# Two u tiles moved behind the convolved channels, first z columns split early, merging stage's loads by chunk

## The chip, the cores and the metric

One core of one Trainium2 chip runs the whole program. The metric is the device time of one execution in microseconds (us), and less is better. TensorE is called PE, VectorE DVE, ScalarE ACT, GpSimd POOL, and SyncE SP; SP only issues transfers.

## What is computed

Two model blocks run one after the other on 1024 tokens of 1024 features, in float32. The change touches the first projection of the first block and the merging stage of the second. Cut to what matters:

```python
# first block: projection of the normed tokens (and of 256 context tokens), 5168 columns
u, zf, zs, xbc, dt_raw = split(h @ w_in)             # 512, 512, 1536, 2560, 48 columns
xbc = silu(depthwise_conv_3x3(xbc) + conv_b)         # 16 x 64 grid of tokens; 3 taps for the context
four = fourier_mixer(u, zf, ...)                     # u as it is, z through silu
# second block: merging
merged = sigmoid(g_fox + b) * (out_fox @ w_proj_fox) + sigmoid(g_dsa + b) * (out_dsa @ w_proj_dsa)
x = x + gate * (merged @ w_out)                      # then norm, scale and shift, and the router
```

## The kernel before

`project_first` holds the normed tokens, turned, in two float32r parts (`hh` high, `hl` low); a product of two split operands takes three matmuls (`three`). Weights are split alike: high is a copy in float32r, low is the raw value less high.

**The channels' stage** (`project_channels`) makes 24 tiles of 128 columns, two for each piece of 256 columns that SP brings into a ring of three buffers (`Ring`) and that POOL splits (`Splits.part`) into one of two weight buffers. POOL may split piece g when both tiles of piece g-2 are summed. Tiles 0 to 3 are the u columns (`scalar_u` copies a sum out and stores it). Tiles 4 to 23 are the channels c = 0 to 19 of xbc: PE sums the tile, ACT copies it into a padded image (`scalar`), DVE makes the nine taps of the grid and three of the context (`vector`), ACT applies silu and stores (`scalar_silu`), PE turns the result in tensor_turn (two tiles later, between the first and second 512 tokens of a sum) and ACT copies that out (`scalar_turn`). Images and results have two buffers each. At the stage's end all engines wait for all of its signals, stores included.

**The z stage** (`project_tokens`) makes 4 groups of 512 z columns by 8 token tiles. SP brings 512 columns (2 MB), ACT splits off high, DVE makes low (`split`), PE sums with hh and hl stationary and the weights moving. Beside it DVE weighs 14 pieces of modulation weights (`weigh`), and PE adds each up with one matmul (`add_up`) after two z tiles. The splits of groups 1 to 3 stand ahead of a `weigh` on DVE.

**The merging stage** (`merge`, some 1,900 us later) works through 8 token tiles: PE projects `oT` (attention results, `ofoxT` and `odsaT`) with `wp`, DVE multiplies by the gates `gs` (POOL adds the bias `bg`, ACT takes the sigmoid), DVE adds both halves (line 2165), PE turns the sum, projects the next tile and closes this one with `wo`. At its start POOL issues the weights' loads (8 MB in three transfers) and SP issues `bg` and four broadcast rows before `oT`, `gs` and `x` of the first tile. Each engine works off its own instructions in the order of the code; nothing reorders them.

Of the kernel before, what the change touches and what calls it, by code (L numbers as in the profile page):

```python
# [357 lines left out]
class Splits:  # L358


    def __init__(self, core, s, ring):
        self.core, self.ring = core, ring
        self.w = [[s.sb(f"w1_{k}{b}", [P, KD, 256], R32) for k in ("high", "low")] for b in range(2)]
        self.halves, self.parted, self.summed = s.sem("w1_high_done"), s.sem("w1_split"), s.sem("xbc_summed")

    def part(self, g):
# [4 lines left out]
        split_on_pool(self.core, self.w[g % 2][0][:], self.w[g % 2][1][:], ring.raw[p % 3][:], self.halves).then_inc(*self.parted.up())  # L371


def project_channels(core, dram, tables, taps, ring, splits, hh, hl, ready):

# [4 lines left out]
    with Stage(core) as s:  # L380
        img = [s.sb(f"img{b}", [P, GRID_H + 2, GRID_W + 2]) for b in range(2)]
        line = [s.sb(f"line{b}", [P, CTX + 2]) for b in range(2)]
        acc, res = ([s.sb(f"{k}{b}", [P, TOK]) for b in range(2)] for k in ("acc", "res"))
        xt = [s.sb(f"xt{b}", [P, NT + NC, P]) for b in range(2)]
        zeroed, evicted, activated = s.sem("img_zeroed"), s.sem("xbc_evicted"), s.sem("xbc_silu_done")
        tapped, conv = s.sem("tap_done"), s.sem("conv_done")
        xturned, xout = s.sem("xt_turned"), s.sem("xt_copied")
# [15 lines left out]
        def tensor(n):  # L403
# [4 lines left out]
            if n >= 6:  # L408
                tensor_turn(n - 6)
            last = part(n, 1, 512, 512)  # L410
            if n >= 4:
# [24 lines left out]
        def scalar_u(n):  # L436
            s_ = n % 2
            act.wait_ge(*summed.at(n + 1))
            if n >= 2:
                act.wait_ge(*u_stored[s_].at(n // 2))  # L440
            act.activation(res[s_][:, 0:SEQ], flat2(core.bank[:, 3 * s_:3 * s_ + 2, :]), ACT.Copy).then_inc(*evicted.up())
            act.wait_ge(*evicted.at(n + 1))
            act.dma_start(dram["uT"][P * n:P * n + P, :], res[s_][:, 0:SEQ]).then_inc(*u_stored[s_].up())

        def scalar(c):
            s_, n = c % 2, c + 4
# [11 lines left out]
        def scalar_silu(c):  # L458
# [5 lines left out]
            else:  # L464
                act.wait_ge(*u_stored[s_].at(2))
# [23 lines left out]

        for g in range(12):  # L490
            if g + 1 < 12:
                splits.part(g + 1)
                if g + 3 < 12:
                    ring.load(ring.PIECES + g + 3, parted.at(g + 1))
            for n in (2 * g, 2 * g + 1):
                tensor(n)
                if n < 4:
                    scalar_u(n)
                else:
                    scalar(n - 4)  # L500
                    if n > 4:
                        scalar_silu(n - 5)
                    vector(n - 4)
        scalar_silu(NCT - 1)
        for c in (NCT - 2, NCT - 1):
            tensor_turn(c), scalar_turn(c)


def project_tokens(core, dram, tables, cs, hh, hl):
# [4 lines left out]
    with Stage(core) as s:  # L514
        raw = s.sb("zw_raw", [P, KD, 512])
        zw = [[s.sb(f"zw_{k}{b}", [P, KD, 512], R32) for k in ("high", "low")] for b in range(2)]
# [3 lines left out]
        aw, acc = [s.sb(f"mod_w{b}", [P, KD // 2, 512]) for b in range(2)], s.sb("mod_acc", [P, 512])  # L520
        bias, out = (s.sb(f"mod_{k}", [1, 512]) for k in ("bias", "out"))
        raw_in, high_done, parted = s.dma("zw_raw_in"), s.sem("zw_high_done"), s.sem("zw_split")
# [6 lines left out]
        def sync(i):  # L529
            if i:  # L530
                sp.wait_ge(*parted.at(i))
            sp.dma_start(raw[:], win[:, :, COL_Z + 512 * i:COL_Z + 512 * i + 512]).then_inc(*raw_in.up())

        def split(i):
            act.wait_ge(*raw_in.at(i + 1))
            if i >= 2:
                act.wait_ge(*summed.at(NT * (i - 1)))
            act.activation(zw[i % 2][0][:], raw[:], ACT.Copy).then_inc(*high_done.up())
            dve.wait_ge(*high_done.at(i + 1))
            dve.tensor_tensor(zw[i % 2][1][:], raw[:], zw[i % 2][0][:].bitcast(F32), ALU.subtract).then_inc(*parted.up())  # L540

        def tensor(n):
            i, m = n // NT, n % NT
            if m == 0:
                pe.wait_ge(*parted.at(i + 1))
            if n >= 4:
                pe.wait_ge(*gated.at(n - 3))
            products(pe, core.bank[:, n % 4, :], [p for k in range(KD) for p in three(
                *(a[:, k, P * m:P * m + P] for a in (hh, hl)), *(a[:, k, :] for a in zw[i % 2]))]).then_inc(*summed.up())
# [12 lines left out]
        def fetch_mod(q):  # L562
            w_name, b_name, _, _, at = mods[q]
            cols = slice(512 * at, 512 * at + 512)
            for half in range(2):
                if q:
                    sp.wait_ge(*weighed.at(KD * q - 4 + 4 * half))
                sp.dma_start(aw[half][:], dram[w_name].rearrange("(p k) n -> p k n", k=KD)[:, 4 * half:4 * half + 4, cols]).then_inc(*aw_in[half].up())
# [19 lines left out]
        def add_up(q):  # L588
            pe.wait_ge(*weighed.at(KD * q + KD))
            if q:  # L590
                pe.wait_ge(*added.at(q))
# [32 lines left out]
        sync(0), split(0), sync(1)  # L624
# [17 lines left out]
def project_first(core, dram, tables):  # L642
    with Stage(core) as s:
        hh, hl = (s.sb(k, [P, KD, TOK], R32) for k in ("h_high", "h_low"))
        cs = s.sb("mod_silu", [P, KD, 3])
        with Stage(core) as s1:
            taps, ring = s1.sb("taps", [P, 10 * NCT]), Ring(core, s1, dram)
            splits = Splits(core, s1, ring)
            ready = front(core, dram, tables, cs, taps, ring, hh, hl, lambda: splits.part(0))
            project_channels(core, dram, tables, taps, ring, splits, hh, hl, ready)  # L650
        project_tokens(core, dram, tables, cs, hh, hl)

# [2106 lines left out]
```

## Time and profile before

| | us |
|---|---|
| median of 3 runs | 3400.55 (3399.44 to 3404.88) |
| profiled execution | 3398.51, span 3396.3 |
| PE busy | 2863.1 (84%) |
| DVE busy | 2118.6 (62%) |
| ACT busy | 1235.3 (36%) |
| POOL busy | 535.3 (16%) |

The span is that of the instructions in one profiled execution; its own device time is 2.2 us longer, and the median of the runs another 2.0 us. The shares are means over stages with different limits, so the time of a change is read in its own stage. All places in time below are us from the start of the span.

### The profile page before, as it was taken

To read this page: it belongs to the slowest core of one execution; us is meant where nothing else is said; L and a number is where in the kernel's file an instruction comes from. 1 tells how busy PE (TensorE), PEld (TensorE's weight loads), DVE (VectorE), ACT (ScalarE), POOL (GpSimd) and SP (SyncE) were. 2 spreads that over 40 slices of the span, in tenths; PEclk is the share of its full clock that TensorE was granted. 3 is DMA by queue.
4 is the path that set the end of the run, shared out by engine and by line. 5 is a ranking of instruction groups with operands and counts; after the bars stand their busy time and mean duration, and the time that the engine had idled before them with its cause. 6 is when DMAs were issued, how large, how long until landed. Compare 5 with 4: busy or idle time off the path is not lost.

```text
span 3396.3 us, 34380 instructions
## 1 busy us (share of the span) xinstructions
PE 2863.1 (84%) x12552; PEld 2126.6 (63%) x12552; DVE 2118.6 (62%) x2906; ACT 1235.3 (36%) x2024; POOL 535.3 (16%) x320
## 2 busy tenths in 40 slices
PE   7999959979588699879889958795988479999992
PEld 3777746755466444468767847684444368888882
DVE  6399945526688523344726979841222479999985
ACT  3122221110366511122224126572211067777772
POOL 1422100000111100001200045452110011111101
PEclk9999979989788799989999969897999689999996
DMA  6333237534455432134442164114324289999995
GB/s 204 102 103 109 88 130 257 192 127 137 164 187 177 159 135 75 44 112 119 114 122 72 72 144 89 26 41 169 117 75 157 97 316 412 416 412 414 412 389 217
DMA packets 259104, 586.24 MB, mean 173 GB/s; under 512 B 27189, under 2 KB 158245, under 8 KB 241650
## 3 DMA queue, kind: packets, MB, share of 16 engines
q1 hardware_dynamic: 185618, 449.00, 36.9%
q0 software_dynamic: 29968, 64.18, 6.4%
q10 hardware_dynamic: 43344, 70.79, 5.6%
q8 instruction: 103, 1.69, 0.2%
q14 instruction: 71, 0.58, 0.1%
HBM read 463.26 MB, written 120.65 MB: 172 GB/s over the span
## 4 chain that ended last, share of the span: by engine, by line


## 5 line engine op out<-in xcount | busy, mean ns | idle before, releaser
L2413 DVE TENSOR_TENSOR e_low<-e_raw,e_high 128x4096 fp32r<-128x4096 f32 x99 | 438.0, 4426 | 69.5 <-ACT e_high L2407 69.4
L2407 ACT ACTIVATE e_high<-e_raw 128x4096 fp32r<-128x4096 f32 x99 | 359.5, 3633 | 32.8 <-DVE live L2364 26.4
L128 PE MATMUL banks<-p_w_high,p_high 128*128 128x512 f32 (+1 forms) x640 | 250.1, 391 | 18.1 <-DVE p_w_low L1526 18.1
L128 PE MATMUL banks<-p_w_low,p_high 128*128 128x512 f32 (+1 forms) x640 | 245.8, 384 | 0.0
L128 PE MATMUL banks<-p_w_high,p_low 128*128 128x512 f32 (+1 forms) x640 | 245.1, 383 | 0.0
L128 PE MATMUL banks<-c_w,c_mT 128*128 128x512 f32 x512 | 225.9, 597 | 9.0 <-DMA c_w<-in_w_out 9.0
L128 PE MATMUL banks<-e_high,e_xhigh 128*128 128x512 f32 x528 | 211.1, 400 | 10.0 <-issue 7.2
L483 DVE SCALAR_TENSOR_TENSOR acc<-img,taps,acc 128x1024 f32<-128x1024 f32 x160 | 209.8, 1311 | 5.7
L128 PE MATMUL banks<-h_high,w_high 128*128 128x512 f32 (+1 forms) x544 | 201.0, 370 | 9.2 <-POOL w_low L355 4.5
L128 PE MATMUL banks<-e_high,e_xlow 128*128 128x512 f32 x528 | 207.9, 394 | 0.0
L128 PE MATMUL banks<-e_low,e_xhigh 128*128 128x512 f32 x528 | 207.2, 392 | 0.0
L128 PE MATMUL banks<-h_low,w_high 128*128 128x512 f32 (+1 forms) x544 | 198.2, 364 | 0.0
L128 PE MATMUL banks<-h_high,w_low 128*128 128x512 f32 (+1 forms) x544 | 198.1, 364 | 0.0
L128 PE MATMUL banks<-m_wp,m_oT 128*128 128x512 f32 x256 | 126.3, 656 | 60.7 <-DMA m_oT<-odsaT 36.0
L128 PEld LDWEIGHTS banks<-c_w,c_mT 128*128 128x128 f32 x512 | 96.5, 192 | 122.8 <-issue 113.1
L1423 DVE TENSOR_SCALAR_CACHE_REDUCE c_rows<-c_rows,i_cand 128x384 bf16<-128x384 f32 (+5 forms) x186 | 169.0, 944 | 2.2
L2544 POOL DMA_INDIRECT e_x<-h,ids x33 | 87.8, 2661 | 500.1 <-PE banks L138 458.2
L1998 POOL TENSOR_TENSOR a_P<-a_P,a_rc 128x256 f32<-128x256 f32 (+7 forms) x64 | 135.1, 2111 | 122.2 <-DVE a_rc L1990 121.6
L128 PEld LDWEIGHTS banks<-p_w_high,p_high 128*128 128x128 f32 x640 | 123.3, 193 | 40.6 <-issue 18.5
L1093 PE MATMUL banks<-s_xf,s_M 128*128 128x64 f32 x768 | 107.3, 305 | 47.9 <-DVE s_M L1050 25.4
L1093 PEld LDWEIGHTS banks<-s_xf,s_M 128*128 128x128 f32 x768 | 107.2, 222 | 59.2 <-issue 26.6
L128 PEld LDWEIGHTS banks<-p_w_high,p_low 128*128 128x128 f32 x640 | 123.1, 192 | 23.9
(452 smaller groups left out, 6127.5 us busy)
## 6 DMA issues: line engine op xcount, KB each, us to landing
e_raw<-in_exp_w SPq DMA_DIRECT2D x99, 2048.0 KB, 10.6
mod_w<-in_ada_w SPq DMA_DIRECT2D x24, 1024.0 KB, 6.1
s_sums<-cumT SPq DMA_DIRECT2D x32, 768.0 KB, 5.2
s_X<-xtok SPq DMA_DIRECT2D x19, 1024.0 KB, 7.4
p_raw<-in_w_in SPq DMA_DIRECT2D x18, 1024.0 KB, 6.5
y<-e_y ACTq DMA_DIRECT2D x33, 512.0 KB, 10.9
xbcT<-res ACTq DMA_DIRECT2D x20, 640.0 KB, 2.9
xtok<-xt ACTq DMA_DIRECT2D x20, 640.0 KB, 3.7
```

Source lines behind the costliest of these rows:

```text
L128: last = pe.matmul(out, a, b, start=start and n == 0, stop=stop and n == len(pairs) - 1)
L483: dve.scalar_tensor_tensor(out=grid, in0=src, scalar=wt, in1=grid, op0=ALU.mult, op1=ALU.add).then_inc(*tapped.up())
L1093: pe.matmul(core.bank[:, y0, HP * h:HP * h + HP], M[n % 2][w][:, h, :], xfs[c % 2][w][:, c0:c0 + HP], start=h == 0 and w == 0, stop=False)
L1423: dve.tensor_scalar(self.junk[n][:, 0:P * (j + 1)], self.score[j], threshold, 0.0, op, ALU.add, accum_out=count).then_inc(*self.found.up())
L1998: pool.tensor_tensor(both, both, over(rc[b][:], 2, L), ALU.mult).then_inc(*scaled.up())
L2407: act.activation(self.high[p % HIGHS][:], self.raw[p % RAWS][:], ACT.Copy).then_inc(*self.high_done.up())
L2413: dve.tensor_tensor(self.low[p % HIGHS][:], self.raw[p % RAWS][:], self.high[p % HIGHS][:].bitcast(F32), ALU.subtract).then_inc(*self.low_ ...
L2544: pool.indirect_dma_start(out=x[b][:], out_offset=None, in_=dram["h2"], in_offset=bass.IndirectOffsetOnAxis(ap=ids[:, m:m + 1].bitcast(U32 ...
```

## The change

In the channels' stage the order of tiles becomes u 0, u 1, channels 0 to 19, u 2, u 3. The ring goes on with pieces 12 and 13, the first 512 z columns; POOL splits piece 12, and after the last u tile ACT and DVE split piece 13 (`split_last`), both into the channels' weight buffers. PE no longer waits at the stage's end, and the z stage starts on those buffers. Later z groups are loaded and split in halves of 256 columns, and the z matmuls read 512 columns as two runs of 256. In the merging stage ACT issues `wp` in 8 chunks of 512 KB and `wo` after the first sigmoid; SP issues `oT` and `gs` of tile 0 first, then `bg`, `x` and the four rows. (A function `fourier` is added that nothing calls.)

```diff
-            col = 256 * g if g < 2 else COL_XBC + 256 * (g - 2)
+            col = 0 if g == 0 else COL_XBC + 256 * (g - 1) if g < 11 else 256 if g == 11 else COL_Z + 256 * (g - 12)
...
+    CONVS = range(2, 2 + NCT)
-    with Stage(core) as s:
+    with Stage(core, (dve, act, pool, sp)) as s:
...
-            if n >= 6:
-                tensor_turn(n - 6)
+            if 4 <= n < 2 * 12 - 1:
+                tensor_turn(n - 4)
...
+        def split_last():
+            act.wait_ge(*ring.here(ring.PIECES + 13))
+            act.wait_ge(*summed.at(24))
+            for k in (0, 4):
+                act.activation(w[1][0][:, k:k + 4, :], ring.raw[(ring.PIECES + 13) % 3][:, k:k + 4, :], ACT.Copy).then_inc(*z_high.up())
+                dve.wait_ge(*z_high.now())
+                dve.tensor_tensor(w[1][1][:, k:k + 4, :], ring.raw[...][:, k:k + 4, :], w[1][0][:, k:k + 4, :].bitcast(F32),
+                                  ALU.subtract).then_inc(*splits.last_split.up())
...
+                if n in CONVS:
+                    scalar(n - 2)
+                    if n > 2:
+                        scalar_silu(n - 3)
+                    vector(n - 2)
+                elif n == 22:
+                    scalar_turn(NCT - 2), scalar_u(n), scalar_silu(NCT - 1)
+                else:
+                    scalar_u(n)
+        split_last()
+        tensor_turn(NCT - 1), scalar_turn(NCT - 1)
...
         def split(i):
-            act.activation(zw[i % 2][0][:], raw[:], ACT.Copy).then_inc(*high_done.up())
-            dve.tensor_tensor(zw[i % 2][1][:], raw[:], zw[i % 2][0][:].bitcast(F32), ALU.subtract).then_inc(*parted.up())
+            for b in range(2):
+                act.activation(zw[i % 2][:, b, 0], raw[b][:], ACT.Copy).then_inc(*high_done.up())
+                dve.tensor_tensor(zw[i % 2][:, b, 1], raw[b][:], zw[i % 2][:, b, 0].bitcast(F32), ALU.subtract).then_inc(*parted.up())
...
-        pool.dma_start(wp[0][:], weights("w_proj_fox_2")).then_inc(*weights_in[0].up())
-        pool.dma_start(wp[1][:], weights("w_proj_dsa_2")).then_inc(*weights_in[1].up())
-        pool.dma_start(wo[:], weights("w_out_2")).then_inc(*weights_in[2].up())
+        for j, name in enumerate(("w_proj_fox_2", "w_proj_dsa_2")):
+            for k in range(4):
+                act.dma_start(wp[j][:, k, :], dram[name][P * k:P * k + P, :]).then_inc(*weights_in[j].up())
...
-        bring(0), bring_x(0)
+        bring(0), bring_x(0), bring_rows()
+        act.dma_start(wo[:], weights("w_out_2")).then_inc(*weights_in[2].up())
```

Three places show the order. The first is ACT from the image of channel 19 to the second z tile; `res` is a silu, `xt` a turned tile, `zo` a z tile. Before:

```order
L454 ACTIVATE img<-banks 128x16x64
L456 ACTIVATE line<-banks 128x256
L466 ACTIVATE res<-acc,taps 128x1280
L468 DMA xbcT<-res 128x1280
L466 ACTIVATE res<-acc,taps 128x1280
L468 DMA xbcT<-res 128x1280
L431 ACTIVATE xt<-banks 128x512 x2
L431 ACTIVATE xt<-banks 128x256
L434 DMA xtok<-xt 128x10x128
```

After the change, from the copy-out of u tile 2 on (`u_out`; `w` is a channels' weight buffer):

```order
L447 ACTIVATE u_out<-banks 128x1024
L449 DMA uT<-u_out 128x1024
L470 ACTIVATE res<-acc,taps 128x1280
L472 DMA xbcT<-res 128x1280
L447 ACTIVATE u_out<-banks 128x1024
L449 DMA uT<-u_out 128x1024
L499 ACTIVATE w<-w_raw 128x1024 x2
L437 ACTIVATE xt<-banks 128x512 x2
L437 ACTIVATE xt<-banks 128x256
L440 DMA xtok<-xt 128x10x128
L582 ACTIVATE zo<-banks 128x512
```

The last silu now stands between two u tiles, and both copies of the z split stand ahead of the last turned tile's copies. The second place is SP at the start of the merging stage, before:

```order
L2108 DMA m_bg<-in_b_gate 128x2048
L2108 DMA m_gate<-mod 128x1024
L2108 DMA m_gain<-in_norm_g 128x1024
L2108 DMA m_m<-mod 128x1024
L2108 DMA m_shift<-mod 128x1024
L2131 DMA m_oT<-ofoxT 128x4x128
L2131 DMA m_oT<-odsaT 128x4x128
L2134 DMA m_gs<-proj 128x2048
```

and after the change:

```order
L2284 DMA m_oT<-ofoxT 128x4x128
L2284 DMA m_oT<-odsaT 128x4x128
L2287 DMA m_gs<-proj 128x2048
L2289 DMA m_bg<-in_b_gate 128x2048
L2300 DMA m_xin<-x 128x1024
L2259 DMA m_gate<-mod 128x1024
L2259 DMA m_gain<-in_norm_g 128x1024
L2259 DMA m_h<-mod 128x1024
L2259 DMA m_shift<-mod 128x1024
L2284 DMA m_oT<-ofoxT 128x4x128
```

The attention results and gates went ahead of 3 MB of broadcast rows, of which 1 MB (`bg`) is still needed before the first gate. The third place is ACT there after the change, where the weights' transfers came in from POOL's queue:

```order
L2253 DMA m_wp<-in_w_proj_fox 128x1024 x4
L2253 DMA m_wp<-in_w_proj_dsa 128x1024 x4
L2294 ACT_TABLE_LOAD
L2294 ACTIVATE m_gs<-m_gs 128x2048
L2380 DMA m_wo<-in_w_out 128x8x1024
L2294 ACTIVATE m_gs<-m_gs 128x2048
```

`wo` stands behind the first sigmoid, which waits for `gs`, `bg` and POOL's add.

## Rows read from the trace of the kernel before

**Rows 1.** By stretch: busy PE, PEld, DVE, ACT, POOL; clock, DMA share, GB/s.
```profile
180.00:413.00 233.00, 222.14 (x1182) 184.27 (x1181) 227.86 (x174) 57.96 (x84) 58.12 (x14) 1.00 0.29 98
...
2350.00:2360.00 10.00, 0.00 (x0) 0.00 (x0) 1.22 (x1) 0.00 (x0) 0.00 (x0) 0.50 1.03 405
```
**Rows 2.** Waits of PE, 485 to 700: us in total, times, longest us.
```profile
PE banks L592 <- DVE mod_acc L586: 9.7, 3, 4.0
```
**Rows 3.** Timeline of PE, 443 to 486: start, us, what, idle before.
```profile
460.76 0.69 PE L138 MATMUL banks<-mats,res 128*128 128x128 f32 x2 [12.77 <-ACT xt L431]
```
**Rows 4.** Timeline of ACT in the channels' stage: copies of sums, silu.
```profile
124.69 1.03 ACT L441 ACTIVATE res<-banks 128x1024 f32<-128x1024 f32 x1 [10.13 <-PE banks L128]
138.70 1.03 ACT L454 ACTIVATE img<-banks 128x1024 f32<-128x1024 f32 x1 [12.98 <-PE banks L128]
...
380.50 1.03 ACT L454 ACTIVATE img<-banks 128x1024 f32<-128x1024 f32 x1 [8.04 <-PE banks L128]
...
401.47 1.36 ACT L466 ACTIVATE res<-acc,taps 128x1280 f32<-128x1280 f32 x1 [3.90 <-DVE acc L487]
413.13 1.03 ACT L454 ACTIVATE img<-banks 128x1024 f32<-128x1024 f32 x1 [8.04 <-PE banks L128]
...
444.29 1.03 ACT L454 ACTIVATE img<-banks 128x1024 f32<-128x1024 f32 x1 [8.08 <-PE banks L128]
```
**Rows 5.** Timelines of DVE and of POOL around one split.
```profile
303.48 0.75 DVE L480 TENSOR_SCALAR acc<-img,taps 128x1024 f32<-128x1024 f32 x1
...
315.10 4.22 DVE L487 SCALAR_TENSOR_TENSOR acc<-line,taps,acc 128x256 f32<-128x256 f32 x2
319.25 5.07 DVE L480 TENSOR_SCALAR acc<-img,taps 128x1024 f32<-128x1024 f32 x1
...
315.38 3.66 POOL L353 TENSOR_TENSOR w_high<-w_raw,zero 128x2048 fp32r<-128x2048 f32 x1 [24.23 <-PE banks L128]
```
**Rows 6.** Timelines of ACT, DVE and PE from the last store to z.
```profile
464.92 0.38 ACTq L434 DMA_DIRECT2D xtok<-xt  x1
477.13 3.62 ACT L538 ACTIVATE zw_high<-zw_raw 128x4096 fp32r<-128x4096 f32 x1 [12.24 <-DMA zw_raw<-in_w_in]
...
480.88 4.42 DVE L540 TENSOR_TENSOR zw_low<-zw_raw,zw_high 128x4096 fp32r<-128x4096 f32 x1 [22.63 <-ACT zw_high L538]
...
485.45 0.77 PE L128 MATMUL banks<-zw_high,h_high 128*128 128x512 f32 x1 [20.98 <-DVE zw_low L540]
```
**Rows 7.** Issues of the merging stage's first loads; then KB, us to landing.
```profile
2340.53 0.35 SPq L2108 DMA_DIRECT2D m_bg<-in_b_gate  x1
...
2343.88 0.50 SPq L2131 DMA_DIRECT2D m_oT<-ofoxT  x1
2344.43 0.55 SPq L2131 DMA_DIRECT2D m_oT<-odsaT  x1
...
m_bg<-in_b_gate SPq DMA_DIRECT2D x1, 1024.0 KB, 5.2
...
m_oT<-ofoxT SPq DMA_DIRECT2D x1, 256.0 KB, 19.1
...
m_oT<-odsaT SPq DMA_DIRECT2D x1, 256.0 KB, 24.7
```
**Rows 8.** Timelines of PE, DVE, ACT and POOL in the merging stage's start.
```profile
2369.22 16.64 PE L128 MATMUL banks<-m_wp,m_oT 128*128 128x512 f32 x32 [35.95 <-DMA m_oT<-odsaT]
...
2391.06 15.88 PE L128 MATMUL banks<-m_wp,m_oT 128*128 128x512 f32 x32
2406.78 13.90 PE L128 MATMUL banks<-m_wo,m_mT 128*128 128x512 f32 x32
...
2387.16 2.09 DVE L2165 TENSOR_TENSOR m_m<-m_m 128x1024 f32<-128x1024 f32 x1
...
2377.78 1.91 ACT L2138 ACTIVATE m_gs<-m_gs 128x2048 f32<-128x2048 f32 x1 [35.68 <-POOL m_gs L2136]
...
2383.66 4.50 POOL L2136 TENSOR_TENSOR m_gs<-m_gs,m_bg 128x2048 f32<-128x2048 f32 x1 [5.91 <-DMA m_gs<-proj]
```

More of the change, by code:

```diff
@@ L362, in __init__ @@
         self.core, self.ring = core, ring
-        self.w = [[s.sb(f"w1_{k}{b}", [P, KD, 256], R32) for k in ("high", "low")] for b in range(2)]
+        self.all = s.sb("w1", [P, 2, 2, KD, 256], R32)
+        self.w = [[self.all[:, b, k] for k in range(2)] for b in range(2)]
         self.halves, self.parted, self.summed = s.sem("w1_high_done"), s.sem("w1_split"), s.sem("xbc_summed")
+        self.last_split = s.sem("z_last_split")
     def part(self, g):
@@ L383, in project_channels @@
         acc, res = ([s.sb(f"{k}{b}", [P, TOK]) for b in range(2)] for k in ("acc", "res"))
+        ur = [s.sb(f"u_out{b}", [P, SEQ]) for b in range(2)]
         xt = [s.sb(f"xt{b}", [P, NT + NC, P]) for b in range(2)]
@@ L488, in vector, with project_tokens @@
                                          in1=acc[s_][:, SEQ:TOK], op0=ALU.mult, op1=ALU.add).then_inc(*(conv if dx == 2 else tapped).up())
+        def split_last():
[4 more added lines that the diff above has]
+                dve.wait_ge(*z_high.now())
+                dve.tensor_tensor(w[1][1][:, k:k + 4, :], ring.raw[(ring.PIECES + 13) % 3][:, k:k + 4, :], w[1][0][:, k:k + 4, :].bitcast(F32),
+                                  ALU.subtract).then_inc(*splits.last_split.up())
         for g in range(12):
[L491 to L494, printed above, removed]
+            splits.part(g + 1)
+            if g + 3 < 14:
+                ring.load(ring.PIECES + g + 3, parted.at(g + 1))
             for n in (2 * g, 2 * g + 1):
                 tensor(n)
-                if n < 4:
-                    scalar_u(n)
[L499 to L509, printed above, removed]
+                if n in CONVS:
+                    scalar(n - 2)
[5 more added lines that the diff above has]
+                else:
+                    scalar_u(n)
+        split_last()
+        tensor_turn(NCT - 1), scalar_turn(NCT - 1)
+    return evicted.now(), xout.now()
+def project_tokens(core, dram, tables, cs, ring, splits, hh, hl, banks_free):
     pe, dve, act, pool, sp = core.pe, core.dve, core.act, core.pool, core.sp
@@ L514, in project_tokens @@
     with Stage(core) as s:
-        raw = s.sb("zw_raw", [P, KD, 512])
-        zw = [[s.sb(f"zw_{k}{b}", [P, KD, 512], R32) for k in ("high", "low")] for b in range(2)]
+        raw = [ring.raw[(ring.PIECES + 12 + b) % 3] for b in range(2)]
+        zw = [splits.all, s.sb("zw", [P, 2, 2, KD, 256], R32)]
         zo = [s.sb(f"zo{b}", [P, 512]) for b in range(4)]
@@ L536, in split @@
-            if i >= 2:
-                act.wait_ge(*summed.at(NT * (i - 1)))
-            act.activation(zw[i % 2][0][:], raw[:], ACT.Copy).then_inc(*high_done.up())
-            dve.wait_ge(*high_done.at(i + 1))
-            dve.tensor_tensor(zw[i % 2][1][:], raw[:], zw[i % 2][0][:].bitcast(F32), ALU.subtract).then_inc(*parted.up())
+            for b in range(2):
+                act.wait_ge(*raw_in[b].at(i))
+                if i >= 2 and b == 0:
+                    act.wait_ge(*summed.at(NT * (i - 1)))
+                act.activation(zw[i % 2][:, b, 0], raw[b][:], ACT.Copy).then_inc(*high_done.up())
+                dve.wait_ge(*high_done.now())
+                dve.tensor_tensor(zw[i % 2][:, b, 1], raw[b][:], zw[i % 2][:, b, 0].bitcast(F32), ALU.subtract).then_inc(*parted.up())
@@ L542, in tensor @@
         def tensor(n):
             i, m = n // NT, n % NT
-            if m == 0:
-                pe.wait_ge(*parted.at(i + 1))
+            if n == 0:
+                pe.wait_ge(*banks_free[0])
+                pe.wait_ge(*splits.parted.at(13))
+            elif m == 0:
+                pe.wait_ge(*parted.at(2 * i))
             if n >= 4:
                 pe.wait_ge(*gated.at(n - 3))
-            products(pe, core.bank[:, n % 4, :], [p for k in range(KD) for p in three(
-                *(a[:, k, P * m:P * m + P] for a in (hh, hl)), *(a[:, k, :] for a in zw[i % 2]))]).then_inc(*summed.up())
+            for k in range(KD):
+                if n == 0 and k % 4 == 0:
+                    pe.wait_ge(*splits.last_split.at(k // 4 + 1))
+                last = products(pe, core.bank[:, n % 4, :].rearrange("p (b n) -> p b n", b=2), three(
+                    *(a[:, k, P * m:P * m + P] for a in (hh, hl)), *(zw[i % 2][:, :, j, k, :] for j in range(2))), start=k == 0, stop=k == KD - 1)
@@ L551, in scalar @@
+            last.then_inc(*summed.up())
         def scalar(n):
@@ L622, in time_steps @@
             dve.tensor_copy(tables["dt"][:].rearrange("p t h -> p (t h)"), core.bank[:, 7, 0:480]).then_inc(*dt_done.up())
-        sync(0), split(0), sync(1)
+        sync(1)
         fetch_mod(0)
```

178 lines of the change are left out of this document (144 added, 34 removed).

## The prediction

> **What bounds the kernel now.** No engine bounds the whole, so I read it by stage. First the busy time by stretch: in the middle of the channels' stage, 180 to 413, DVE is busy 227.9 of 233 us and PE 222.1 [rows 1]. Both are close to full, DVE the closer. Then the timeline of POOL beside that of DVE, for why DVE is so full. The reader is to see the same instruction, the first tap at line 480, take 0.75 us at 303.48 and 5.07 us at 319.25, and the two context taps take 4.22 us where POOL's split starts at 315.38 [rows 5]. While POOL splits, those DVE instructions stand still. ACT's timeline gives the pace that follows: with a split in a pair of channels the pair takes 413.13 - 380.50 = 32.6 us, and without one, where PE is the limit, 444.29 - 413.13 = 31.2 us [rows 4].
>
> Then the seam to the z stage. PE's last sum of the channels ends just before ACT's copy at 444.29 [rows 4]. The first z product starts at 485.45 [rows 6]. Between them PE waits 12.8 us for DVE and ACT to finish the last channel [rows 3] and 21.0 us for the z weights [rows 6]: their load could only be issued when the store issued at 464.92 had landed, it was there at 477.13, and the split took until 485.3 [rows 6]. So 41.2 us pass, with only the transposes of two tiles in them, and these 41 us are what the change goes for. After it the z stage is PE's own but for 9.7 us in three waits for the modulation sums [rows 2].
>
> Last the start of the merging stage: PE stands until 2369.22 for odsaT [rows 8], with the DMA engines full at 405 GB/s [rows 1]. PE starts as early as the bytes ahead of it allow.
>
> **The change, channels' stage.** The first channel takes the place of u tile 2 on PE. ACT's copy of u tile 2 had begun at 124.69 - 10.13 - 1.03 = 113.5 [rows 4]; a channel has a context part more, which is 138.70 - 124.69 = 14.0 against 11.2 for a u tile, so 2.85 us. Its image is then at 113.5 + 2.9 = 116.4 instead of 138.7: **22.3 us earlier**, and with it DVE's whole chain. The new order does not shorten DVE's work. It lengthens it: POOL now splits two more pieces while channels are convolved (piece 11 at channel 17, piece 12 at channel 19). Each costs DVE 5.07 - 0.75 = 4.3 us at line 480 and 4.22 - 1.0 = 3.2 us at the context taps, 7.5 us in all [rows 5]; the 1.0 for two short taps is an estimate, from 0.75 us for four times the columns. What of it shows is less, since the pair of channels 18 and 19 had been PE's. I take the image of channel 17 at 413.13 - 22.3 = 390.8 and add a pair with a split, 32.6: the image of channel 19 at 423.4, not 422.0.
>
> PE then sums u tiles 2 and 3, 11.2 us each, with the transposes of channel 18 between. Those cost 1.6 us, what a pair without a split has over two channels: (31.2 - 2 x 14.0) / 2. So 423.4 + 22.3 + 1.6 = 447.3. Under these tiles the last convolution ends: silu of channel 15 came 401.47 - 380.50 = 21.0 us after its own image with a split in between [rows 4], so silu of channel 19 starts at 444.4. The cover is only 2.9 us long. If DVE were later than that, PE's last transposes and the z start would be late by the rest.
>
> **The seam after the change.** Piece 13 is split into the buffer that u tile 3 read, so ACT cannot begin before 447.3. In ACT's order stand the copy of u tile 3 (1.03), its store's issue (0.4), two copies of 1,024 columns (a quarter of 3.62 is 0.9 each, 1.03 by the nearest copy [rows 6, 4]), and then the copy of channel 19's first turned columns (0.6). PE's last two transposes wait for that copy, since they reuse its bank, and z stands behind them. z starts at 447.3 + 1.0 + 0.4 + 2.0 + 0.6 + 0.7 = 452.0. The 0.7 are those two transposes and the hand-overs. DVE's low part of the first four blocks (a quarter of 4.42, 1.1 us) is done by 451. So the z start moves from 485.45 to 452.0: **-33.4 us**. The stage's end, which PE used to wait for, is now only waited for by the others: the last store, issued at about 453, lands some 4 us later, and ACT's first z tile is not summed before 458.
>
> **Inside the z stage.** Three splits of a group each stand ahead of a weigh on DVE. Before, ACT 3.62 and DVE 4.42 us came one after the other, 8.0 us [rows 6]; in halves DVE starts after 1.8 us and runs 4.4, 6.3 us. Each of the three waits shrinks by 1.8 of its 4.0, 2.9 and 2.9 (sum 9.7 [rows 2]): -5.4, and I add 0.6 for the clock that PE keeps: **-6 us**. Between nothing and -9.7. The loads of z columns 512 on are issued at 457 and are 2 MB of 400 GB/s, so there by 466, when ACT reaches their split. Extra issues (0.4 us each on SP, six) lie under PE.
>
> The z matmuls read two runs of 256 columns 16 KB apart, 768 times. No row shows that form. From below nothing, since the column count is the same. From above, as if each were two matmuls of 256: those cost 2.85 / 24 = 119 ns each, 238 for two, against 11.16 / 48 = 232 ns for one of 512 [rows 4], so +5 us at most by rows. I take nothing.
>
> **The merging stage.** `oT` of tile 0 was issued at 2343.88 and 2344.43 and landed at 2363.0 and 2369.1, so the second 256 KB took 6.1 us beside the weights of the other queue [rows 7]; alone at 405 GB/s it would have been 0.6. In these 6.1 us some 2.5 MB passed, 2.2 of them weights. After the change `oT` goes first on SP and `wp`, 4 MB, goes beside it from ACT. I take the same sharing: two pieces at 6.1 us are 12.2 us, in which the 4 MB also pass (4.7 MB at 400 is 11.8 us). Data flow from 2342.9: `bg`, 1 MB, was issued at 2340.53 and landed 5.2 later [rows 7], and 2.6 of that are its bytes; until then there is the same start. So PE starts at 2355 instead of 2369.2. Bounds: 2349, if `oT` slips through at once and the first half of `wp` with it; 2363, if both queues drain before `oT`.
>
> From there PE is no longer alone on the path. `gs` and `bg` follow, 1 MB each at 2.6 us: 2360.3. POOL's add takes 4.5, ACT's sigmoid 1.9 [rows 8]: gates at 2366.8, earlier than PE's 2371.6 (2355 + 16.6 [rows 8]), so hidden by 4.8 us. DVE's second product and the sum (1.2 each) end at 2374.1, transposes at 2376. `oT` of tile 1 is behind 2.5 MB more on SP, 6.7 us: 2367 to 2374, the later if `wo`, issued at 2366.8, is beside it. It is hidden, by 2 us at least. PE's second projection (15.9) ends at 2392 against 2406.8: **-14.8 us**. `wo` (4 MB from 2368.5, shared with 1.5 MB) is in by 2384, needed at 2392. ACT's copies of the turned sum stand behind the second sigmoid, 2384.5 to 2386, also before 2392. The gain row, now made behind the first tile's products, lies under PE's close.
>
> One thing speaks against the full amount. The sum at line 2165, which reads two tensors in SBUF, took 2.09 us where POOL's add ran from 2383.66 to 2388.16 [rows 8]: it ended 1.1 us after the add. `gs` of tile 1 lands near 2373, and the sum is due at 2372.9. If the add comes first, the sum ends at 2378.4 and the gain is 10.5. I take **-14 us**, between the two and near the full one. The Trainium skill, "SBUF — State Buffer", section "SBUF: two separate sides", says that the port pair of DVE and GpSimd is an exclusive lock held for the whole instruction, also against a DVE operation with two SBUF inputs. By that rule the late add costs its whole rest, 10.5 of gain in place of 14.8, and each further split costs the convolution its whole length; the trace agrees, with 5.07 us for 0.75.
>
> **Sum.** -33.4 - 6 - 14 = -53.4. On the profiled execution's 3398.5 that is 3345.1; the median of the runs stands 2.0 above it, so **3347**. Everything after each of the two places keeps its length.
>
> **Rivals.** *The merging stage gives little* (16 in 100): the small pieces of `oT`, 512 bytes each, wait for all the weights, 2363, and the sum falls behind POOL's add. Then 6.2 - 4.3 = 2 to 6 us are left: 3355 to 3359. For it: the second piece took 6.1 us beside weights; against it: that very time is in my sum.
>
> *The seam gives less* (15 in 100): DVE needs the 7.5 us of a further split in full, or the doubled z read costs its 5 us, or `split_last` is slower on ACT. DVE's cover of 2.9 us is gone and 5 to 7 us come back: 3352 to 3356. For it: DVE busy at 227.9 of 233. Against it: the two u tiles are the cover, and 22 us long.
>
> *Slower* (4 in 100): the z matmul with its moving operand in two runs streams at half the rate. 768 at 232 ns more are +178 us: 3525. It decides from 53.4 / 768 = 70 ns a matmul on: above 302 ns each, the kernel is slower. No row speaks for it, and none rules it out, since the form is not in the trace.
>
> *Both stages short together* is 3 in 100, 3361 to 3366. My own forecast holds the other 62, with 3337 to 3354 as its own range (upper end: gain of 10.5 in merging and 3.5 less in z; lower end: 18 in merging, all 9.7 in z, 2 more for a better clock after a shorter wait).
>
> **Range and chances.** 3336 to 3361 leaves out the slower case, both short, and a part of the first rival and of my own tails. 0.2% is 6.8 us, about what a measurement of this kernel can tell from no change. Faster by more: all but the slower case and a little for what I don't see, 0.95. Same 0.01, slower 0.04.
>
> **What would show it.** In the profile after: first image copy near 116.5; channel 19's near 423; last u copy near 447; first z product 450 to 454, its wait 3 to 4 us in place of 12.8 and 21.0 us; PE's waits in z for the modulation sums near 4 us in all; z matmuls still at 232 ns apart; from the z stage on all starts 40 us earlier. In the merging stage PE's first product comes 14 to 15 us after SP's first issue in place of 28.7, `wo`'s first 51 to 53 after it in place of 66.2. I am wrong if PE's wait before z is over 6 us, if DVE is still convolving when u tile 3 is summed, or if the first projection starts over 20 us after that issue.

## The result, and the profile after

| | before | after |
|---|---|---|
| median | 3400.63 (3399.44 to 3404.88) | 3348.95 (3347.65 to 3354.00) |
| profiled execution | 3398.51, span 3396.3 | 3348.61, span 3347.0 |

The ratio of the two is 0.9849, with a 95% interval of 0.9832 to 0.9866: 51.7 us less. The forecast was 3347 (3336 to 3361).

**The channels' stage after**, ACT's timeline (start us, us), against [rows 4]:

```profile
91.65 1.03 ACT L447 ACTIVATE u_out<-banks 128x1024 f32<-128x1024 f32 x1 [1.01 <-POOL h_low L337]
119.02 1.03 ACT L460 ACTIVATE img<-banks 128x1024 f32<-128x1024 f32 x1 [19.90 <-PE banks L128]
...
426.19 1.03 ACT L460 ACTIVATE img<-banks 128x1024 f32<-128x1024 f32 x1 [8.06 <-PE banks L128]
447.13 1.37 ACT L470 ACTIVATE res<-acc,taps 128x1280 f32<-128x1280 f32 x1 [6.98 <-DVE acc L491]
450.36 1.03 ACT L447 ACTIVATE u_out<-banks 128x1024 f32<-128x1024 f32 x1 [1.86 <-PE banks L128]
451.84 2.00 ACT L499 ACTIVATE w<-w_raw 128x1024 fp32r<-128x1024 f32 x2 [0.46 <-ACT u_out L447]
```

Forecast were 116.4 for the first image, 423.4 for that of channel 19, 444.4 for its silu and 447.3 for the last u tile. All came 2.6 to 3.1 us later, so the distances between them held within 0.5 us: the cover of 2.9 us over the last convolution was 3.2. The stage before ended late, as the first row shows (91.65; 89.09 in the trace of before). DVE's timeline shows the further splits as priced, 4.23 and 5.07 us [rows 5]:

```profile
425.61 0.35 DVE L488 TENSOR_SCALAR acc<-line,taps 128x256 f32<-128x256 f32 x1
426.00 4.23 DVE L491 SCALAR_TENSOR_TENSOR acc<-line,taps,acc 128x256 f32<-128x256 f32 x2
430.15 5.07 DVE L484 TENSOR_SCALAR acc<-img,taps 128x1024 f32<-128x1024 f32 x1
```

**The seam and the z stage**, PE's timeline, against [rows 3, 6]; then PE's waits in z, against [rows 2]:

```profile
454.38 0.44 PE L138 MATMUL banks<-mats,res 128*128 128x128 f32 x2 [3.19 <-ACT xt L437]
454.58 0.71 PE L128 MATMUL banks<-w,h_high 128*128 128x512 f32 x2
```

```profile
PE banks L617 <- DVE mod_acc L612: 4.9, 3, 2.4
```

The whole z stage in one stretch of each kernel, first product to last copy-out, before and then after:

```profile
485.45:698.39 212.94, 203.22 (x800) 149.17 (x801) 103.40 (x131) 30.07 (x35) 0.00 (x0) 0.96 0.62 207
```

```profile
454.58:657.31 202.73, 197.87 (x802) 145.87 (x802) 104.41 (x135) 30.93 (x40) 0.00 (x0) 0.99 0.67 221
```

The first number behind the stretch is its length, the next PE's busy time, and the third from the end the granted clock (1.00 is 2.4 GHz, 0.50 is 1.2). Not only are 4.9 us of waits gone (212.94 - 203.22 = 9.7 before, 4.9 after): the same matmuls also took 5.3 us less, at a clock of 0.99 in place of 0.96. The operand in two runs cost nothing that shows.

The clock by stretches says where most of these 5.3 us lie. Six us at the end of the second wait before (2.9 us), and at the end of the longest one after (2.4 us):

```profile
568.00:574.00 6.00, 5.78 (x16) 3.84 (x17) 1.25 (x3) 0.00 (x0) 0.00 (x0) 0.72 1.04 392
```

```profile
479.00:485.00 6.00, 3.83 (x14) 2.44 (x15) 2.72 (x4) 0.39 (x1) 0.00 (x0) 1.00 1.07 370
```

Before, the stretch at each of the three waits (4.0, 2.9 and 2.9 us) shows 0.72, which is up to 1.7 us lost each time. After, none of the three waits (2.4, 1.2 and 1.2 us) is followed by a fall.

**The merging stage**: PE, DVE, POOL and ACT. SP's first issue is at 2302.13 (before 2340.53), and places are told from there, as +16.1:

```profile
2318.27 9.23 PE L128 MATMUL banks<-m_wp,m_oT 128*128 128x512 f32 x16 [23.42 <-DMA m_wp<-in_w_proj_fox]
2328.41 7.13 PE L128 MATMUL banks<-m_wp,m_oT 128*128 128x512 f32 x16 [0.91 <-DMA m_wp<-in_w_proj_dsa]
2338.12 1.09 PE L138 MATMUL banks<-mats,m_m 128*128 128x128 f32 x8 [2.58 <-DVE m_m L2321]
2341.93 16.22 PE L128 MATMUL banks<-m_wp,m_oT 128*128 128x512 f32 x32 [2.72 <-DMA m_oT<-odsaT]
2357.99 13.90 PE L128 MATMUL banks<-m_wo,m_mT 128*128 128x512 f32 x32
```

```profile
2336.84 1.23 DVE L2321 TENSOR_TENSOR m_m<-m_m 128x1024 f32<-128x1024 f32 x1
```

```profile
2344.46 4.50 POOL L2292 TENSOR_TENSOR m_gs<-m_gs,m_bg 128x2048 f32<-128x2048 f32 x1 [20.63 <-DMA m_gs<-proj]
```

```profile
2323.86 1.91 ACT L2294 ACTIVATE m_gs<-m_gs 128x2048 f32<-128x2048 f32 x1 [15.61 <-POOL m_gs L2292]
2323.87 0.39 ACTq L2380 DMA_DIRECT2D m_wo<-in_w_out  x1
```

PE starts at +16.1, where 14.5 was forecast and 28.7 stood before [rows 8]. It does not wait for what the forecast had it wait for: `odsaT` of tile 0 landed at +9.6, and the row names `wp`, whose first half was in at +16.1 and whose second at +26.3. DVE's sum is not held up, since POOL's second add comes after it. But `oT` of tile 1, forecast for +26.5 to +33.5 and called hidden, landed at +39.8, and PE waited 2.7 us. PE's clock by stretches shows what else that pause cost:

```profile
2337.00:2340.00 3.00, 1.09 (x8) 0.86 (x8) 1.06 (x1) 0.00 (x0) 0.00 (x0) 0.94 1.04 392
2340.00:2343.00 3.00, 1.07 (x2) 0.55 (x3) 0.00 (x0) 0.00 (x0) 0.00 (x0) 0.50 1.07 415
2343.00:2346.00 3.00, 3.00 (x5) 1.29 (x4) 0.00 (x0) 0.00 (x0) 1.54 (x1) 0.50 1.05 349
2346.00:2349.00 3.00, 3.00 (x8) 1.21 (x7) 0.00 (x0) 0.01 (x1) 2.96 (x1) 0.93 1.00 370
```

The clock is at its lower level (0.50) from 2340 to 2346, and the projection takes 16.22 us where one without a pause takes 13.90. `wo`'s first product comes at +55.9, against 66.2 before: 10.4 us, not 14.

### The profile page after: what moved, and what is told of

It is laid out like the page before. It is cut to its first block, busy times and chain, and to the rows that moved or that the text cites. A ratio compares the mean times of both kernels' runs of the same rounds, so it can differ in the third digit from the quotient of the medians.

```text
span 3347.0 us, 34406 instructions
## 1 busy us (share of the span) xinstructions
PE 2859.2 (85%) x12552; PEld 2116.9 (63%) x12552; DVE 2136.1 (64%) x2910; ACT 1232.7 (37%) x2028; POOL 540.7 (16%) x319
## 4 chain that ended last, share of the span: by engine, by line
## 5 line engine op out<-in xcount | busy, mean ns | idle before, releaser
L2566 ACT ACTIVATE e_high<-e_raw 128x4096 fp32r<-128x4096 f32 x99 | 359.5, 3633 | 32.8 <-DVE live L2523 26.5
L128 PE MATMUL banks<-h_high,w 128*128 128x512 f32 (+1 forms) x1088 | 309.1, 367 | 9.0 <-POOL w L356 4.4
L128 PEld LDWEIGHTS banks<-h_high,w 128*128 128x128 f32 x1088 | 195.4, 190 | 48.9 <-POOL w L356 4.8
L128 PE MATMUL banks<-h_low,w 128*128 128x512 f32 (+1 forms) x544 | 198.5, 365 | 0.0
```

The costliest lines, as they stand in the source:

```text
L128: last = pe.matmul(out, a, b, start=start and n == 0, stop=stop and n == len(pairs) - 1)
L2566: act.activation(self.high[p % HIGHS][:], self.raw[p % RAWS][:], ACT.Copy).then_inc(*self.high_done.up())
```

## The experiments

All times are medians; the kernel before ran 3399.1 to 3400.6 beside them. Ratios are to that kernel on the same chip. Columns: distances in each trace, from ACT's first u copy (first number) to the first z product; the z stage; from there to SP's first issue of the merging stage; from that issue to PE's first and to `wo`'s first product.

| | median | ratio | copy | to z | z | between | PE | wo |
|---|---|---|---|---|---|---|---|---|
| before | 3400.6 | | 89.1 | 396.4 | 212.9 | 1642.1 | 28.7 | 66.2 |
| after | 3348.9 | 0.9849 | 91.7 | 362.9 | 202.7 | 1644.8 | 16.1 | 55.9 |
| e1 channels only | 3357.8 | 0.9885 | 91.5 | 362.3 | 204.3 | 1641.6 | 28.0 | 64.9 |
| e2 merge only | 3387.2 | 0.9967 | 91.2 | 396.2 | 211.5 | 1642.3 | 20.8 | 54.2 |
| e3 u first | 3363.2 | 0.9889 | 91.1 | 376.2 | 204.4 | 1647.8 | 15.9 | 56.6 |
| e4 order only | 3388.3 | 0.9966 | 90.3 | 381.8 | 211.6 | 1648.1 | 28.5 | 66.3 |
| e5 wo late | 3346.5 | 0.9840 | 91.8 | 363.2 | 202.7 | 1650.5 | 15.8 | 54.9 |
| e6 rows late | 3346.5 | 0.9845 | 91.3 | 362.7 | 204.2 | 1644.4 | 16.2 | 48.9 |
| e7 wo early | 3350.7 | 0.9853 | 90.7 | 362.9 | 202.7 | 1648.3 | 16.2 | 56.0 |
| e8 ACT high | 3341.0 | 0.9822 | 92.1 | 351.3 | 203.7 | 1649.7 | 15.7 | 55.2 |
| e9 e6 and e8 | 3335.7 | 0.9811 | 91.4 | 350.6 | 202.9 | 1645.5 | 15.7 | 50.6 |
| e10 after again | 3350.6 | 0.9849 | 92.8 | 362.2 | 204.3 | 1648.0 | 15.9 | 56.8 |
| e11 wp whole | 3341.6 | 0.9828 | 90.5 | 362.8 | 202.7 | 1646.8 | 13.1 | 48.5 |
| e12 wp on POOL | 3350.2 | 0.9854 | 90.8 | 363.1 | 202.7 | 1643.7 | 19.1 | 57.7 |

The columns "between" and "copy" are noise, and they set how far one trace can be read. "Between" has the same work in all 14 and runs from 1641.6 to 1650.5. "Copy" is 90.3 to 92.8 in 13 of them, e2 among them, whose code is that of before up to there: the 89.09 of before was the odd one. The column "z" is steadier, and its steps are the clock's: behind the 2.4 us wait it fell in six of the eleven traces with the new stage (e1, e3, e5, e6, e9, e10) and stayed at 1.00 in five (after, e7, e8, e11, e12), and one fall costs 1.6 us, as from 202.7 to 204.3 (e5 and e9 regain it at the start, where they alone have 1.00).

### The two stages apart

e1 is the changed kernel with the old `merge`, e2 the old kernel with the new `merge`.

> The change with the merging stage of before. My theory: the channels' stage, the seam and the z stage give their part alone, and the two places do not act on each other. Then the time is 3349 plus the 10.4 us by which the merging stage's first product with wo came closer to that stage's start, 3359 to 3360; z start near 452 to 455, merging stage's first issue near 2301. Rival: part of the gain is shared (each hides the other's wait), and the time is over 3364.

> The kernel before with the new merging stage. My theory: 3400.6 - 10.4 = 3390, with the first projection 16 us after the stage's first issue and the first product with wo 56 us after it, as in the changed kernel. It also says whether the front of the program is as in before (first u copy at 89.1) or 2.6 us later as in the changed kernel (91.7): if later here too, that shift is chance and not the ring's new place. Rival: the merging stage's gain needs the earlier stages' new timing, and the time stays at 3400.

e1 is 42.0 us faster than its kernel before, e2 12.6, together 54.6 against 51.7: they add, as far as intervals of 5 to 6 us on each can tell.

In e2 the merging stage did not start as forecast: PE began at +20.8 and not at +16, and still reached `wo` at +54.2, earlier than the changed kernel. `oT` of tile 1 had landed when the second projection came, so there was no pause and that projection took 13.90 us in place of 16.22. The rows of ACT's issue of the first `wp`, in the changed kernel and in e2 (SP's first issue at 2302.13 and 2341.15):

```profile
2302.14 2.65 ACTq L2253 DMA_DIRECT2D m_wp<-in_w_proj_fox  x4
```

```profile
2341.44 5.13 ACTq L2104 DMA_DIRECT2D m_wp<-in_w_proj_fox  x4
```

In e2 ACT's first issue is 0.3 us behind SP's, not 0.01, and `odsaT` took 3.7 us to land in place of 9.2. In the eight traces with an offset of 0.01 us and `wp` in pieces, `odsaT` takes 8.9 to 9.6 us and PE starts at +15.7 to +16.2. So the start of this stage can come out in two ways with the same instructions; whether the 0.3 us make the difference was not tested.

### The order and the early split apart

e3 keeps the early split and puts all u tiles first again; e4 has the new order and the old z stage.

```diff
-            col = 0 if g == 0 else COL_XBC + 256 * (g - 1) if g < 11 else 256 if g == 11 else COL_Z + 256 * (g - 12)
+            col = 256 * g if g < 2 else COL_XBC + 256 * (g - 2) if g < 12 else COL_Z + 256 * (g - 12)
...
-    CONVS = range(2, 2 + NCT)
+    CONVS = range(4, 4 + NCT)
```

(This is e3's against the changed kernel; e4's is that of the change without pieces 12 and 13, `split_last` and the halves.)

> The change with all four u tiles ahead of the channels again, but z still split early into the channels' buffers. My theory: DVE's last convolution has no cover. It ends where it did before, near 458, the silu and the last turned tile follow, and z starts near 462 to 465 and not at 454.6: 8 to 10 us slower than the changed kernel, 3357 to 3359. Rival: the order of tiles is worth nothing once z is split early, because the convolutions' total is the same; then 3349.

> The kernel before with only the order of tiles changed (u 2 and u 3 behind the channels), z loaded and split as before, after the stage's end. My theory: the last sum ends near 447 to 450, the last store lands some 6 us later, the z load takes 8 us and its split 8 us, so z starts near 470 to 473 in place of 485.45: 13 to 15 us faster than before, 3386 to 3388. Rival: without the early split the order gives back all of it, since the load waits for the stage's end; then 3400.

PE's timeline, in e3 and then in e4:

```profile
463.93 0.69 PE L138 MATMUL banks<-mats,res 128*128 128x128 f32 x2 [12.19 <-ACT xt L437]
```

```profile
450.92 0.44 PE L138 MATMUL banks<-mats,res 128*128 128x128 f32 x2 [1.30 <-ACT xt L433]
472.18 0.77 PE L128 MATMUL banks<-zw_high,h_high 128*128 128x512 f32 x1 [20.82 <-DVE zw_low L540]
```

Each leaves just the wait that the other removes: 12.2 us for the last channel in e3, 20.8 us for the z weights in e4. From the first copy to z the early split alone is worth 20.2 us and the order alone 14.6; both together 33.5. e4 came as forecast, with z at 472.18. e3 missed its range by 4 us: z started at 467.3, not at 462 to 465, so the missing cover costs 13.3 us (376.2 against 362.9), not 8 to 10. The rest of its trace's difference, 3.0 us between z and merging, is noise.

### What made `oT` of tile 1 late

e5 issues `wo` behind the second sigmoid, e6 issues the four rows behind `oT` and `gs` of tile 1, e7 issues `wo` right behind `wp`.

```diff
-        bring(0), bring_x(0), bring_rows()
+        bring(0), bring_x(0)
...
                 bring(n + 1)
+            if n == 0:
+                bring_rows()
```

(e6; in e5 the line that issues `wo` stands at that place, and in e7 right behind the loop over `wp`.)

> The merging stage gained 10.4 us where 14 were forecast. PE's second projection began 39.8 us after SP's first issue of the stage, after a wait of 2.7 us for odsaT of tile 1 (forecast: landed 26 to 34 us after it). Here wo is issued by ACT behind the second sigmoid, so that oT and gs of tile 1 have the DMA engines nearly alone. Theory: oT(1) was late because it shared the engines with the 4 MB of wo. Then oT(1) lands 26 to 29 us after the first issue, the wait of 2.7 us is gone, gs(1) lands near 32, POOL's add comes ahead of DVE's sum or beside it, wo's first product comes near 53 us after the first issue in place of 55.9, and the time is 2.5 to 5 us below the changed kernel's 3348.9: near 3345. Rival: oT(1) waits for the bytes ahead of it on its own queue (bg, x and the four rows), whatever ACT sends: no change, 3348 to 3350, and the wait stays.

> The four broadcast rows of 512 KB each, which nothing needs before DVE's close of tile 0, are issued behind oT and gs of tile 1; wo stays where it is. Theory (sharing with wo by packets): oT(1) has 2 MB less ahead of it on SP's queue and lands 5 to 8 us earlier, 32 to 34 us after SP's first issue, so the 2.7 us wait of PE's second projection goes: 3345 to 3346.5. The rows then land 45 to 50 us after the first issue and DVE needs them near 72. Rival (the bytes of wo in front decide): oT(1) moves by less than 3 us and the time stays at 3348 to 3350.

> wo is issued right behind the eight pieces of wp, not behind the first sigmoid. wp needs the engines until about 25 us after the first issue anyway, and wo follows on the same queue. Theory: placing wo's issue behind the sigmoid is worth little, since the sigmoid comes when wp is nearly through: oT(1) lands 38 to 42 us after the first issue, PE's wait for it stays at 2 to 4 us, 3347.5 to 3351. Rival: the delay of wo is what lets bg and gs of tile 0 through; without it they and oT(1) are 3 us or more later, and the time rises to 3352 or more.

`odsaT` of tile 1 landed at +39.8 in the changed kernel (34.0 us behind its issue), at +29.8 in e5 (24.1) and at +24.6 in e6 (20.8). In e7 nothing moved (+39.9, a wait of 3.0 us): ACT's queue was busy with `wp` until +26.3 anyway. So both are shown: `oT` of tile 1 stands behind 2 MB of rows on its own queue, and beside `wo`. e6 moved it by more than its forecast of +32 to +34. e5 won only 1.0 us for `wo`'s first product all the same. DVE's, POOL's and PE's timelines of e5:

```profile
2342.67 3.51 DVE L2321 TENSOR_TENSOR m_m<-m_m 128x1024 f32<-128x1024 f32 x1
```

```profile
2340.60 4.50 POOL L2292 TENSOR_TENSOR m_gs<-m_gs,m_bg 128x2048 f32<-128x2048 f32 x1 [10.60 <-DMA m_gs<-proj]
```

```profile
2346.24 1.97 PE L138 MATMUL banks<-mats,m_m 128*128 128x128 f32 x8 [4.86 <-DVE m_m L2321]
```

With `gs` of tile 1 there earlier, POOL's add ran from 2340.60 to 2345.10 and the sum, due at 2342.67, ended at 2346.2: 3.51 us in place of 1.23. This is the wait that the prediction had weighed and that the late `gs` had kept away. The Trainium skill, "SBUF — State Buffer", section "SBUF: two separate sides", has the port pair as a lock held to the instruction's end; by that rule the sum would start at 2345.1 and end at 2346.3, and the trace agrees, with 2346.2. In e6 the add came early enough (+27.5 to +32.0) and the sum at +33.0, and PE's row shows no pause of its own:

```profile
2336.87 1.09 PE L138 MATMUL banks<-mats,m_m 128*128 128x128 f32 x8 [2.58 <-DVE m_m L2321]
2337.79 13.90 PE L128 MATMUL banks<-m_wp,m_oT 128*128 128x512 f32 x32
2351.53 13.90 PE L128 MATMUL banks<-m_wo,m_mT 128*128 128x512 f32 x32
```

`wo` is reached 7.0 us earlier in this trace: 1.7 of them before the transposes (no wait of 0.9 us for the second half of `wp`, and 15.43 us of products in place of 16.36), 2.9 at the pause, and 2.3 in the projection behind it, 13.90 for 16.22. In e9 against e8 it is 4.6 (50.6 and 55.2). By the medians e6 is worth only 2.5, with ratios that overlap (0.9827 to 0.9863 against 0.9832 to 0.9866), so its size stays open.

### The pieces, and the queue

```diff
-            for k in range(4):
-                act.dma_start(wp[j][:, k, :], dram[name][P * k:P * k + P, :]).then_inc(*weights_in[j].up())
+            act.dma_start(wp[j][:], weights(name)).then_inc(*weights_in[j].up())     # e11
```

e12 keeps the pieces and lets POOL issue them.

> The changed kernel itself, as the base for the others of this job on the same chip: 3346 to 3351. If the 2.6 us by which its first stage ended late in the first profile was chance, the first image lies anywhere from 116.4 to 119.5 here; if it belongs to the change, at 119 again.

> wp comes in two transfers of 2 MB on ACT's queue, as before in size, in place of eight of 512 KB; all the order is kept. It tells whether the pieces or the order make the merging stage's gain. Theory: the order; bytes come in one after the other on a queue either way, so PE's first product comes 15.5 to 17 us after SP's first issue and the time stays within 1.5 us of the changed kernel's. Rival: the pieces do something themselves (eight in flight share the engines more evenly, or the two halves come in beside each other when they are whole): PE's first product 20 us or more after the first issue, +3 us.

> The eight pieces of wp are issued by POOL, as the whole tensors were before; order and sizes are those of the changed kernel. It tells whether the queue makes part of the gain. The issues cost POOL 0.8 to 0.9 us each, and the first one goes out 0.5 us after SP's. Theory: the order of SP's own queue gives the gain, and POOL's eight issues (7 us, the bytes of four pieces take 5.2) nearly keep up: PE's first product 16 to 19 us after the first issue, +0 to +2 us on the time. Rival: the queue of POOL delivers in another way (before, its 4 MB of wp were in by 22 us beside 4 MB of rows), PE's first product at 20 us or later, +4 us or more.

e11, from which I expected nothing, is the second largest gain of a single edit by its ratio, behind e8: 3341.59 against 3350.60 of e10 on the same chip, with no run of one inside the range of the other; the ratios are 0.9828 (0.9813 to 0.9843) and 0.9849 (0.9836 to 0.9863). My theory was wrong, and on the side that I had not named. PE, and POOL's first add:

```profile
2315.92 16.65 PE L128 MATMUL banks<-m_wp,m_oT 128*128 128x512 f32 x32 [20.38 <-DMA m_oT<-odsaT]
2335.15 1.97 PE L138 MATMUL banks<-mats,m_m 128*128 128x128 f32 x8 [2.58 <-DVE m_m L2320]
2336.91 14.62 PE L128 MATMUL banks<-m_wp,m_oT 128*128 128x512 f32 x32
2351.37 13.90 PE L128 MATMUL banks<-m_wo,m_mT 128*128 128x512 f32 x32
```

```profile
2323.80 4.50 POOL L2291 TENSOR_TENSOR m_gs<-m_gs,m_bg 128x2048 f32<-128x2048 f32 x1 [18.66 <-DMA m_bg<-in_b_gate]
```

The issues with their median time to landing (KB, us), in the changed kernel (the last two pieces of the first `wp`) and then e11, `oT` of tile 0:

```profile
m_wp<-in_w_proj_fox ACTq DMA_DIRECT2D x2, 512.0 KB, 12.9
m_oT<-odsaT SPq DMA_DIRECT2D x1, 256.0 KB, 9.2
```

```profile
m_wp<-in_w_proj_fox ACTq DMA_DIRECT2D x1, 2048.0 KB, 10.6
m_oT<-odsaT SPq DMA_DIRECT2D x1, 256.0 KB, 12.6
```

(In both, ACT's first issue goes out with SP's.) In pieces `odsaT` took 9.2 us and PE then waited for `wp` until +16.1. Whole, the first `wp` was in after 10.6 us and `odsaT` after 12.6: ACT's queue got more of the engines beside the same queue of SP, and the two ended 2.4 us apart, the later at +13.1. The issues of the pieces were not the limit: the four of the first `wp` went out within 2.7 us, the first landed at +4.4 and the last at +16.1. The pieces bring nothing for it, since PE waits for all four anyway. `wp` was also through at +21.2, and `wo` went out only at +25.5 (the sigmoid waited longer for `bg`), so that SP's queue was alone for 4 us; `odsaT` of tile 1 landed at +29.4 and the pause was gone. The Trainium skill, "DMA: Bandwidth & Descriptors", section "Queues, rings and completion order", says that an engine takes turns between queues by whole packets of descriptors. No run here shows how these packets were made up. The profile's own count on ACT's queue, from 2285 to 2420, is 2768 in the changed kernel and 2672 in e11 for the same 10.49 MB: 16 fewer for each of the six transfers saved, so the rows moved are as long. Why the whole transfers got more stays open. e11 has one profiled execution, and e2 shows that the start of this stage can turn out in another way; the gain itself rests on the medians.

In e12 PE starts at +19.1, 3 us later than with ACT's queue, while SP's things came sooner (`odsaT` 4.3 us after its issue). That this is POOL's queue is not shown: its first issue goes out 0.5 us behind SP's, and e2, with ACT's queue 0.3 us behind, has the same picture (3.7 us, +20.8). The pause is missing here too, and the median is that of e10.

### Half of the split taken from POOL

```diff
+                if c % 2 == 0:
+                    splits.high_on_act(n // 2 + 1)
+                    splits.low_on_pool(n // 2 + 1)
             act.wait_ge(*summed.at(n + 1))
```

> In the channels' stage ACT makes the high halves of the weight pieces (one copy of 2,048 columns, 1.9 us, between a turned copy and the eviction) and POOL only the low ones, so POOL holds DVE for about half as long. Theory: DVE's pair of channels takes 32.6 us only through POOL's split (a first tap of 0.75 us takes 5.07, the context taps 4.2); with half the split the pair takes PE's 31.2, ten pairs give 12 to 14 us at the image of channel 19, and all behind it is that much earlier: 3335 to 3338. Rival 1: PE is the next limit at once and ACT's copies hold up PE's transposes and banks, by 1 to 1.9 us a pair: nothing gained, 3345 to 3352. Rival 2: the pair was bound by PE and ACT already and POOL's lock was hidden: 3347 to 3350.

The images of channels 17 and 19 are 31.3 us apart, where a pair took 32.6 [rows 4]:

```profile
383.77 1.03 ACT L476 ACTIVATE img<-banks 128x1024 f32<-128x1024 f32 x1 [8.08 <-PE banks L128]
...
415.05 1.03 ACT L476 ACTIVATE img<-banks 128x1024 f32<-128x1024 f32 x1 [8.06 <-PE banks L128]
```

DVE still stands behind POOL's low half (14.78 us here, 10.53 for the same eight taps without it), but for 4.3 us in place of 7.5, and now waits for ACT 1.9 us in each pair:

```profile
385.11 0.75 DVE L500 TENSOR_SCALAR acc<-img,taps 128x1024 f32<-128x1024 f32 x1 [1.89 <-ACT line L478]
385.90 14.78 DVE L503 SCALAR_TENSOR_TENSOR acc<-img,taps,acc 128x1024 f32<-128x1024 f32 x8
```

z starts 11.6 us earlier, against 12 to 14 forecast; the median is 8 us lower, and at 3341.0 it is 3 us above its range. Busy times from 180 to 413 show who is the next limit:

```profile
180.00:413.00 233.00, 229.24 (x1219) 192.08 (x1218) 214.48 (x181) 74.75 (x97) 40.08 (x8) 1.00 0.35 117
```

PE is at 229.2 us of 233 (222.1 before) and DVE at 214.5 (227.9) [rows 1]. So the time that POOL's split takes from DVE is shown as the limit of the channels' stage, with PE's 31.2 us right behind it.

> Both gains of the second job together: ACT makes the high halves in the channels' stage (image of channel 19 11.1 us earlier in the trace) and the four broadcast rows go behind oT and gs of tile 1 (wo's first product 48.9 us after SP's first issue of the merging stage in place of 55.9, and 1037.0 in place of 1044.9 us from that issue to the end of the span). The two places are 1,850 us apart. Theory: they add, 18.1 us by the traces: 3330.8, and 3328 to 3335 with the middle of the kernel as uneven as seen (it took 1838 to 1847 us in seven traces with the same work). Rival, by the timed medians (7.9 and 2.5): 3338.5. The image of channel 19 should come near 415, wo's first product 49 us after the first issue.

e9 ran 3335.68 (3330.60 to 3338.70), 14.9 below e10: between the two forecasts, and just over the range of the first. It is the fastest version run, with a ratio of 0.9811 (0.9797 to 0.9824). Whole `wp` with ACT's high halves was not run.

## Why the prediction was right

The median is 1.9 us from the forecast. The seam, the largest term, was right in its mechanism and its size; that the rest came out too is in part luck.

- **The seam**, -33.4: -33.5 (396.4 to 362.9). Every step held within 0.5 us, and e3 and e4 show the two waits that it was made of.
- **The z stage**, -6: -10.2 in this pair of traces, -8.6 over all (212.0 in three traces with the old stage, 203.4 in eleven with the new). "Each of the three waits shrinks by 1.8" was right within 0.2 us: 4.9 us less, 5.4 forecast. Mis-sized is "I add 0.6 for the clock that PE keeps": that term was 5.3 us in these two traces and 3.7 over all. The clock fell behind seven of the nine waits of 2.9 us and more in the three traces with the old stage, at about 1.7 us each (one at 3.4), and behind none of the waits of 1.2 us.
- **The merging stage**, -14: -10.4. "So PE starts at 2355" is 1.6 us short and has the wrong transfer: the sum let both pieces of `oT` take 6.1 us each and all 4 MB of `wp` pass in those 12.2 us. In the trace `oT` was there by +9.6, and PE waited for `wp`, of which 2 MB were in by +16.1. The near hit is luck. (The sum's 2342.9 for the start of the data is 2343.1 from the rows; this changes nothing.) "It is hidden, by 2 us at least", of `oT` of tile 1, failed outright: it came 6 us after the later bound, a pause of 2.7 us. That bound had `wo` beside it, but took SP's rows for bytes at the full rate while two queues shared the engines. e5 and e6 each removed the pause. The lock on DVE, for which 0.8 us was taken off, did not strike here; it struck in e5.
- So the three terms give -54.1 in place of -53.4, two errors of some 4 us against each other. The 2.6 us at the first copy and 2.7 us between come back on top; by e2 and the column "between" they are chance. The profiled execution is therefore 3.5 us above its forecast of 3345.1. The median is nearer because it stands 0.3 us above the profiled execution after the change, not 2.0 as was added.
- **Rivals.** "The merging stage gives little" did not occur in either of its conditions: `oT` did not wait for all the weights, and the sum did not fall behind POOL's add. "The seam gives less" and the doubled matmul did not occur.

## What to carry to other kernels

Price a reordering of loads to the second consumer, not the first: the start came 12.6 us earlier, and 2.2 of these went again by `wo`'s first product. Price a wait with what the clock loses behind it: here 1.7 us on top of 2.9. A load cut in pieces helps only where the consumer waits for each piece, and beside another queue it got less than the whole in e11's pair. Compare traces by distances between marks, since 1,640 us of unchanged work differed by up to 9 us here.

## What had not been expected of the hardware

- Eight transfers of 512 KB got less of the DMA engines beside SP's queue than two of 2 MB: the first 2 MB landed at +16.1 and at +10.6. The same pieces landed at +20.8 in e2.
- A wait of 2.4 us was followed by a fall of PE's clock in six of eleven traces of the same code, and not in the other five.
- A pause of PE of 2.7 us, after one of 2.6, cost 2.3 us more behind it (16.22 for 13.90), the granted clock being 0.50.
- A transfer that ACT issues behind an activation goes at that one's start (2323.87, activation from 2323.86 to 2325.77), so "behind the sigmoid" means when the sigmoid begins. In e5 and e11 the two also start 0.01 us apart.
